# Weight slots with two k tiles interleaved element by element (stationary operand at a stride of 8 bytes)

## What is computed

```
xn = rmsnorm(x) * norm_gain
rq, rk, rv, rg, sq, sk, sv, sg, gr, gs = split(xn @ w_in)        # w_in is 2048 x 14336
o_ret = retention(rope(rq), rope(rk), rv)      # 8 heads, chunks of 128, states in and out
o_sb  = stick_breaking(sq, sk, sv)             # 8 heads, prompt keys or paged cache keys
h = x + (sig(gr) * ((GN(o_ret) * silu(rg)) @ w_ret) + sig(gs) * ((o_sb * silu(sg)) @ w_sb)) @ w_out
y = rmsnorm(h) * final_gain
```

## Time and profile before

| | |
|---|---|
| runs | 2050.27, 2048.37, 2047.24 us |
| span of the profiled execution | 2046.7 us |
| PE busy | 2016.3 us (99%) |
| PEld (weight loads) busy | 1961.5 us (96%) |
| VectorE busy | 1536.7 us (75%) |
| ScalarE busy | 995.5 us (49%) |
| HBM | 135 GB/s over the span |

### The profile page before, as it was taken

How to read it: one execution, slowest core, us unless ns; L and a number is a source line. 1 busy time by engine, 2 the same in 40 slices (tenths; PEclk the granted TensorE clock), 3 DMA queues, 4 the chain that set the end, 5 groups by cost and what they waited for, 6 DMA issues and landing times.

```text
span 2046.7 us, 42371 instructions
## 1 busy us (share of the span) xinstructions
PE 2016.3 (99%) x15572; PEld 1961.5 (96%) x15572; DVE 1536.7 (75%) x2053; ACT 995.5 (49%) x1458; POOL 111.3 (5%) x133
## 2 busy tenths in 40 slices
PE   7999999999999999999999999999999999999996
PEld 6999999999999999999999999999999999999996
DVE  6977777777772377878888888888887755468886
ACT  5546555556563355444554454555555632234343
POOL 0022221122200000000000000000000000000000
PEclk8999999999999999999999999999999999999998
DMA  4445555555554444334344334333446354544444
GB/s 159 133 137 150 149 158 145 143 154 147 149 163 146 131 124 151 95 107 118 105 123 128 95 113 130 115 117 110 124 139 214 120 156 151 172 151 111 120 125 139
DMA packets 456803, 277.23 MB, mean 135 GB/s; under 512 B 20739, under 2 KB 436867, under 8 KB 455555
## 3 DMA queue, kind: packets, MB, share of 16 engines
q1 hardware_dynamic: 454532, 271.22, 45.0%
q10 hardware_dynamic: 2176, 4.72, 0.6%
HBM read 235.76 MB, written 40.11 MB: 135 GB/s over the span
## 4 chain that ended last, share of the span: by engine, by line
PE 93%; DVE 3%; DMA 1%; DVEq 1%; ACT 1%; issue 0%; SPq 0%; ACTq 0%
PE ACC L796 44%; PE ACC L802 22%; PE ACC L702 14%; PE Z L722 4%; PE Z L942 1%; PE Z L921 1%; PE Z L832 1%; DMA RAW<-in_w_ret_proj 1%; PE ACC L748 1%; PE ACC L1249 1%; PE Z L1022 1%; PE Z L848 0%; DVE TTL L2416 0%; PE Z L1037 0%; DMA XN<-in_x_prompt 0%
## 5 line engine op out<-in xcount | busy, mean ns | idle before, releaser
L1326 ACT ACTIVATE HI<-RAW 128x1024 fp32r<-128x1024 f32 x434 | 447.1, 1053 | 561.3 <-DVEq L1895 326.2
L1872 DVE TENSOR_TENSOR LO<-RAW,HI 128x1024 fp32r<-128x1024 f32 x434 | 535.9, 1240 | 149.3 <-ACT HI L1326 117.5
L796 PE MATMUL ACC<-XH,HI 128*128 128x288 f32 x1728 | 471.3, 299 | 0.0
L796 PE MATMUL ACC<-XL,HI 128*128 128x288 f32 x1728 | 464.3, 294 | 0.0
L796 PE MATMUL ACC<-TH,HI 128*128 128x288 f32 x1296 | 358.6, 303 | 0.0
L796 PE MATMUL ACC<-TL,HI 128*128 128x288 f32 x1296 | 352.0, 296 | 0.0
L796 PEld LDWEIGHTS ACC<-XH,HI 128*128 128x128 f32 x1728 | 324.4, 188 | 17.8 <-issue 11.7
L796 PEld LDWEIGHTS ACC<-XL,HI 128*128 128x128 f32 x1728 | 324.5, 188 | 0.0
L802 PE MATMUL ACC<-XH,LO 128*128 128x288 f32 x1728 | 264.0, 294 | 0.0
L796 PEld LDWEIGHTS ACC<-TH,HI 128*128 128x128 f32 x1296 | 243.7, 188 | 4.4 <-ACT HI L1326 2.3
L796 PEld LDWEIGHTS ACC<-TL,HI 128*128 128x128 f32 x1296 | 243.7, 188 | 0.0
(11 more groups left out here) (376 smaller groups left out, 3136.7 us busy)
## 6 DMA issues: line engine op xcount, KB each, us to landing
RAW<-in_w_in SPq DMA_DIRECT2D x224, 512.0 KB, 4.0
RAW<-in_w_out SPq DMA_DIRECT2D x33, 512.0 KB, 4.5
KV<-in_cache_sb_k SPq DMA_DIRECT2D x256, 64.0 KB, 1.9
KV<-in_cache_sb_v SPq DMA_DIRECT2D x256, 64.0 KB, 1.9
RAW<-in_w_ret_proj SPq DMA_DIRECT2D x32, 512.0 KB, 4.2
RAW<-in_w_sb_proj SPq DMA_DIRECT2D x16, 512.0 KB, 4.0
ST<-in_state_ret SPq DMA_DIRECT2D x64, 128.0 KB, 2.6
out<-ST SPq DMA_DIRECT2D x64, 128.0 KB, 1.9
```

The costliest lines, as they stand in the source:

```text
L796: mm = pe.matmul(to, HI[:, w, k, :], x[:, k, :], start=k == 0 and x is xh, stop=False)
L1326: act.activation(HI[:, SLOT[pos]], RAW[:, SRC[n]], ACT.Copy).then_inc(S["hi_made"], 1)
L1872: dve.tensor_tensor(LO[:, SLOT[pos]], RAW[:, SRC[n]], HI[:, SLOT[pos]].bitcast(F32), ALU.subtract)\
```

## The change

The slots of HI and LO have the same size in the same place, but k tile k and k tile k + 4 of a slot are interleaved: element n of both stand beside each other. A view with the axes (slot, half j, k, n) is made of the buffer, and every user takes its tile from this view. The columns of a stationary tile then stand 8 bytes apart. RAW, the operands x, the number and the order of instructions and all waits are as before.

```diff
-        HI, _ = sb("HI", [P, 3, 8, P], F32R)
-        LO, _ = sb("LO", [P, 3, 8, P], F32R)
+        HI_B, _ = sb("HI", [P, 3, 4, P, 2], F32R)
+        LO_B, _ = sb("LO", [P, 3, 4, P, 2], F32R)
+        HI, LO = [b[:, :, :, :, :].rearrange("p s k n j -> p s j k n") for b in (HI_B, LO_B)]
...
+        def halves(ap):
+            return ap.rearrange("p (j k) n -> p j k n", j=2)
...
-                            mm = pe.matmul(ACC[a][:, half, 0:HALF], w[:, s // 2, s % 2 * QK + k, :],
+                            mm = pe.matmul(ACC[a][:, half, 0:HALF], w[:, s // 2, s % 2, k, :],
...
-                        mm = pe.matmul(to, HI[:, w, k, :], x[:, k, :], start=k == 0 and x is xh, stop=False)
+                        mm = pe.matmul(to, HI[:, w, k // 4, k % 4, :], x[:, k, :], start=k == 0 and x is xh, stop=False)
...
-                    mm = pe.matmul(to, LO[:, w, k, :], xh[:, k, :], start=False, stop=k == 7)
+                    mm = pe.matmul(to, LO[:, w, k // 4, k % 4, :], xh[:, k, :], start=False, stop=k == 7)
...
-                act.activation(HI[:, s // 2, s % 2 * QK:(s % 2 + 1) * QK, :], RAW[:, r, (n % 2) * QK:(n % 2 + 1) * QK, :],
+                act.activation(HI[:, s // 2, s % 2, :, :], RAW[:, r, (n % 2) * QK:(n % 2 + 1) * QK, :],
                                ACT.Copy).then_inc(S[f"hi_full{s}"], 1)
...
-                act.activation(HI[:, SLOT[pos]], RAW[:, SRC[n]], ACT.Copy).then_inc(S["hi_made"], 1)
+                act.activation(HI[:, SLOT[pos]], halves(RAW[:, SRC[n]]), ACT.Copy).then_inc(S["hi_made"], 1)
...
-                part = slice(s % 2 * QK, (s % 2 + 1) * QK)
-                dve.tensor_tensor(LO[:, s // 2, part, :], RAW[:, r, (n % 2) * QK:(n % 2 + 1) * QK, :],
-                                  HI[:, s // 2, part, :].bitcast(F32), ALU.subtract).then_inc(S[f"w_full{s}"], 1)
+                dve.tensor_tensor(LO[:, s // 2, s % 2, :, :], RAW[:, r, (n % 2) * QK:(n % 2 + 1) * QK, :],
+                                  HI[:, s // 2, s % 2, :, :].bitcast(F32), ALU.subtract).then_inc(S[f"w_full{s}"], 1)
...
-                dve.tensor_tensor(LO[:, SLOT[pos]], RAW[:, SRC[n]], HI[:, SLOT[pos]].bitcast(F32), ALU.subtract)\
+                dve.tensor_tensor(LO[:, SLOT[pos]], halves(RAW[:, SRC[n]]), HI[:, SLOT[pos]].bitcast(F32), ALU.subtract)\
                     .then_inc(S["lo_made"], 1)
```

More of the change, by code:

```diff
@@ L747, in first_tile @@
                             for w, x in ((HI, XH), (HI, XL), (LO, XH)):
-                                mm = pe.matmul(ACC[0][:, half, 0:HALF], w[:, q // 2, q % 2 * QK + k, :],
+                                mm = pe.matmul(ACC[0][:, half, 0:HALF], w[:, q // 2, q % 2, k, :],
                                                x[:, 4 * q + k, half * HALF:(half + 1) * HALF],
@@ L1248, in _ @@
                     for x in (xh, xl):
-                        pe.matmul(to, HI[:, w, k, :], x[:, k, :], start=k == 0 and x is xh, stop=False)
+                        pe.matmul(to, HI[:, w, k // 4, k % 4, :], x[:, k, :], start=k == 0 and x is xh, stop=False)
                 if pos == 5:
```

## The result

The changed kernel takes 2054.85 us (median of 11 runs, 2050.49 to 2056.94) against 2048.76 us for the kernel before in 11 runs: a ratio of 1.0025, 95% interval 1.0017 to 1.0032. (The medians lie 6.1 us apart, 0.30%; the means of the same runs lie 4.9 us apart, 0.24%.) The profiled execution took 2051.91 us with a span of 2049.7 us, so 3.0 us more of span than before; it is one of the quicker of its kernel. Another profiled execution of the same kernel (first experiment) has a span of 2051.1 us.

The account below looks back on a forecast made before the run. TensorE was taken as the bound: 13,104 matmuls at a 131 ns pitch set by moving columns, 84% of the span. Span 2046.7 + 0 for the change + 1.7 to the median gave 2048.4 us, range 2036 to 2195 us.

Parts of the forecast that it names:

- small growth of HI and LO, or a fraction of a ns in pitch: Case of the forecast slower by a little than the 0.2% that can be told; chance 0.06.
- Step (1): 13,104 weight loads at 8 bytes: 116 ns each, hidden under the 131 ns pitch, 0 us; upper bound +1166 us.
- load-bound rival: Stride-8 load passes 131 ns and becomes the pitch of all 13,104 matmuls; up to 3215 us, chance 0.12.
- Step (2): Moving stream disturbed or relieved by the load beside it: -11 to +11 ns per matmul, -144 to +144 us; taken as 0.
- My own mark for a wrong prediction: A matmul pitch off by 0.3 ns or more in either direction makes the prediction wrong.
- Step (3): ScalarE writing HI and VectorE writing LO at stride 8: unchanged, 0 us; if doubled, about +340 us through VectorE.
- The point from which it decides: VectorE's free time, 2.7 us in a pair: growth of 0.39 us on each LO (+31%).
- supply rival: VectorE's strided LO passes 1.6 us and TensorE waits for LO in every pair; up to 2390 us, chance 0.07.
- relief: Faster rival: spreading a tile over twice the addresses thins a load-stream clash; -11 ns each, down to 1904 us, chance 0.09.

Follow-up runs that it names:

- first experiment: The changed kernel run again with no edit, beside three runs that take it apart: 2053.25 us, ratio 1.0026.
- e2: On the kernel before, only TensorE's weight loads read at a stride of 8 bytes, makers write contiguously: 2050.45 us, ratio 1.0009.
- e8: Kernel before with a second measuring stretch ahead, strides and tile starts varied between clock-keeping matmuls; only the stretch is read: 128-column load 111.7 ns at 4 bytes, 118.1 at 8.
- e3: On the kernel before, only ScalarE and VectorE write and read HI and LO at 8 bytes, TensorE's loads stay contiguous: 2050.19 us, ratio 1.0007.
- e4: On the changed kernel, ScalarE makes the HI of a product in storage order, reading RAW in pairs 2048 bytes apart: 2061.66 us, ratio 1.0061.
- e5: Kernel before with a measuring stretch (the bench) ahead, strides of loads, moving operands and copies varied: 288-column pitch 131.6 ns at 4 bytes, 133.3 with tile at 8.

## Why the prediction came out as it did

The forecast of 2048.4 us was 0.3% low. The direction that I held likeliest, no change to be told, had its edge at 0.2%; the measured 0.25% (0.17 to 0.32) is the small case beside it, "small growth of HI and LO, or a fraction of a ns in pitch". Of these, HI grew and the pitch moved; LO did not grow. That the number fits so well is in part luck: in the two profiles of the change, +5 and +6 us in the other stages stood beside -2 us in w_ret, which the prediction did not see and the change need not have made.

Step (1), the loads: right, and right in size. I set 116 ns from the sweep of the moving operand against 21 ns of cover; it is 118.1. The pitch that makes the cover was read from counts in windows as 131 ns, some 2 ns too low; the starts give 133, and with the load at 111.7 the cover was 21 ns all the same. The load-bound rival was worth its chance: at 12 bytes it would already have been true. The estimate's ground was luckier than its number, though. A moving operand at 8 bytes takes 255.6 ns for 288 columns, so the moving stream can't sweep twice the bytes, and nothing I read from it had to hold for the load.

Step (2), the moving stream beside the load: the mechanism is there and its size is small. In the bench 131.6 becomes 133.3 ns, in stick-breaking 133.03 becomes 133.25, in the gates 132.94 becomes 133.33, in retention 132.92 becomes 133.36. I took 0 of a range of -11 to +11. By stages of e2 this is some +3.6 us. How the stride does it is not shown; the series of e8 show only that a start 8 bytes later does about as much. My own mark for a wrong prediction was 0.3 ns, and the gates and retention passed it, as did w_ret the other way (1.66 ns). Over all the matmuls of 288 columns the mean moved by 0.03 ns (133.07 to 133.10), since w_ret, the start and w_out cancel most of it. By that mark the step "I take 0" failed in the stages, although the sum did not show it.

Step (3), the makers: this term was mis-sized. LO was right (1240 ns). For HI I read from the earlier trace rows that a broken pattern costs nothing, but those rows break into runs of 8 elements, each contiguous; they hold no stride between elements. The copy grew by 10% in place of 0. I had priced a few per cent as 19 waits of 0.1 us, 2 us together. e3 measures +1.5 us, so the sum was near; its way was another: not many waits growing by one copy, but one place per retention head growing by three copies, 8 x 0.23 = 1.8 us, of which some 0.5 us is given back by shorter waits up to 17 matmuls further on. In e4 the same place grows by 0.72 us with three copies that are 0.25 us longer each. The point from which it decides was set on VectorE's occupancy (0.39 us on each LO), while the chain that binds runs through ScalarE's latency.

The supply rival with VectorE as its bound, and relief, did not come. Relief's -144 us has not even a shadow, since w_ret's quicker rhythm came with contiguous loads too.

What stays open: whether the two edits together cost more (4.6 to 6.1 us by the medians) than the sum of what they cost apart (1.8 and 1.5), and why the changed kernel's runs scatter from 2050 to 2057 us where most of the others stay within 3 us. The spans of the profiled executions add up: +0.9 us in e2 and +2.2 in e3, +3.0 and +4.4 in the two of the change. The first of those two was among the quicker of its runs (the third of 11), the second in their middle (2053.30 us, median 2053.25).

## What to carry to other kernels

Find what hides a transfer or a load and how much of the cover is left before pricing a stride: here 8 bytes left 15 ns of 21 and kept the load hidden, 12 bytes would have cost some 40 ns on each of 13,104 matmuls (an estimate from the 174.7 ns of e5). Price a maker's op by its place in a chain, not by its engine's busy share: ScalarE is half idle, and its 0.1 us counted three times at one place per head, where TensorE waited before too. Before giving a stage's gain to a change, look at the same stage in every trace that lacks the change: w_ret ran at 130.00 ns once with no stride at all. And a row is only evidence for a pattern if it holds that pattern: runs of eight say nothing of a stride between elements.

## What the runs showed of the hardware

The moving operand (fp32r) did not tolerate the stride: 288 columns at 8 bytes take 255.6 ns at a granted clock of 1.00, where contiguous ones take 131.6, while a stationary tile at 8 bytes costs the load 6.4 ns.

VectorE is unmoved by 8 bytes on the written side, on one of the two it reads, or on both (1226 ns), and ScalarE pays for it (1056 to 1117 ns); from 16 bytes on both need 1.9 to 2.0 ns per element.

A TensorE that the profile calls busy can lose its clock. In e5, matmuls of 64 columns held back by their own loads (111.7 ns apart, then some 118; PE 100% busy by the profile) were followed by a fall of the granted clock from 1.00 to 0.50, the lower of its two levels. It came back during the 256-column series. What made it fall no run takes apart. The windows are of 64 columns with the tile at 4 and at 12 bytes, and of 256 columns at 8 bytes:

```profile
40.30:43.80 3.50, 3.50 (x33) 3.47 (x32) 0.00 (x0) 0.00 (x0) 0.00 (x0) 1.00 0.00 0
49.20:56.00 6.80, 6.80 (x34) 6.80 (x33) 0.00 (x0) 0.00 (x0) 0.00 (x0) 0.50 0.00 0
126.20:129.80 3.60, 3.60 (x32) 3.60 (x31) 0.00 (x0) 0.00 (x0) 0.00 (x0) 1.00 0.00 0
```
